# Attention of a two-layer diffusion backbone: two head pairs per step instead of one

## What is computed

```python
s_loc = jnp.einsum('bjqhd,bjlhd->bhjql', qr, kr).astype(jnp.float32) * scale + bias[None]
s_ctx = jnp.einsum('bjqhd,bnhd->bhjqn', qr, ctx_k).astype(jnp.float32) * scale
p = jax.nn.softmax(jnp.concatenate([s_loc, s_ctx], axis=-1), axis=-1)
o = jnp.einsum('bhjql,bjlhd->bjqhd', p[..., :L].astype(vr.dtype), vr)
o = o + jnp.einsum('bhjqn,bnhd->bjqhd', p[..., L:].astype(ctx_v.dtype), ctx_v)
```

## Time and profile before

| | before |
|---|---|
| median of 3 runs | 1589.21 us (1588.29 to 1589.9) |
| the profiled execution's own time | 1589.82 us |
| its span | 1588.0 us |
| TensorE busy (matmul, weight loads) | 99%, 87% |
| DVE, ACT, POOL busy | 83%, 49%, 25% |
| granted TensorE clock | 0.9 or more of full speed in all 40 slices |

### The profile page before, as it was taken

How to read it: one execution, slowest core, us unless ns; L and a number is a source line. 1 busy time by engine, 2 the same in 40 slices (tenths; PEclk the granted TensorE clock), 3 DMA queues, 4 the chain that set the end, 5 groups by cost and what they waited for, 6 DMA issues and landing times.

```text
span 1588.0 us, 28228 instructions
## 1 busy us (share of the span) xinstructions
PE 1567.4 (99%) x9688; PEld 1387.7 (87%) x9688; DVE 1313.5 (83%) x2295; ACT 772.5 (49%) x1443; POOL 389.5 (25%) x302
## 2 busy tenths in 40 slices
PE   7999999999999999999999999999999999999998
PEld 6788898789999999888878879977899999998886
DVE  7899787668999999966669987876699999998575
ACT  6433235538655555524383323363775555563333
POOL 0042012001555555300000600120035555541000
PEclk9999999999999999999999999999999999999999
DMA  9444375051222222454414444812412223235451
GB/s 363 140 131 158 99 270 164 14 146 54 79 81 79 85 88 85 152 161 163 149 40 146 142 131 155 276 61 87 76 66 80 83 89 92 80 93 180 126 186 66
DMA packets 66221, 195.05 MB, mean 123 GB/s; under 512 B 15444, under 2 KB 16852, under 8 KB 65880
## 3 DMA queue, kind: packets, MB, share of 16 engines
q1 hardware_dynamic: 50840, 175.54, 34.9%
q10 hardware_dynamic: 15296, 18.39, 3.6%
HBM read 187.05 MB, written 6.85 MB: 122 GB/s over the span
## 4 chain that ended last, share of the span: by engine, by line
PE 86%; DVE 7%; issue 3%; ACT 1%; DVEq 0%; ACTq 0%
PE bank L2155 12%; PE bank L2156 12%; PE bank L2157 12%; PE bank L2673 10%; PE bank L2674 10%; PE bank L2672 10%; PE bank L2311 2%; PE bank L2313 2%; PE bank L2315 2%; DVE ada_sq L1387 2%; PE bank L2467 2%; PE bank L2453 2%; DVE w_lo L1376 1%; PE bank L2177 1%; PE bank L2441 1%
## 5 line engine op out<-in xcount | busy, mean ns | idle before, releaser
L788 ACT ACTIVATE w_hi<-raw 128x1024 fp32r<-128x1024 f32 (+1 forms) x120 | 123.1, 1029 | 379.2 <-PE bank L2157 297.4
L1376 DVE TENSOR_TENSOR w_lo<-raw,w_hi 128x1024 fp32r<-128x1024 f32 (+1 forms) x128 | 154.3, 1213 | 113.6 <-ACT w_hi L788 113.2
L2155 PE MATMUL bank<-w_hi,aT_lo 128*128 128x512 f32 x520 | 210.3, 404 | 2.7 <-DVE aT_lo L1840 2.5
L2156 PE MATMUL bank<-w_lo,aT_hi 128*128 128x512 f32 x520 | 205.7, 396 | 0.0
L2157 PE MATMUL bank<-w_hi,aT_hi 128*128 128x512 f32 x520 | 205.2, 395 | 0.0
L2672 PE MATMUL bank<-aT_hi,w_lo 128*128 128x322 f32 x640 | 198.9, 311 | 0.7 <-DVE u L2020 0.7
L2673 PE MATMUL bank<-aT_lo,w_hi 128*128 128x322 f32 x640 | 199.4, 312 | 0.0
L2674 PE MATMUL bank<-aT_hi,w_hi 128*128 128x322 f32 x640 | 198.7, 310 | 0.0
L1268 ACT ACTIVATE w_hi<-raw 128x512 fp32r<-128x512 f32 x200 | 118.0, 628 | 147.4 <-POOL raw L668 139.4
L2155 PE MATMUL bank<-w_hi,m_lo 128*128 128x512 f32 x400 | 158.5, 396 | 0.0
L2156 PE MATMUL bank<-w_lo,m_hi 128*128 128x512 f32 x400 | 157.3, 393 | 0.0
(11 more groups left out here) (292 smaller groups left out, 3866.0 us busy)
## 6 DMA issues: line engine op xcount, KB each, us to landing
raw<-in_stream SPq DMA_DIRECT2D x304, 512.0 KB, 3.7
lead<-in_lead SPq DMA_DIRECT2D x16, 512.0 KB, 12.0
bias<-in_bias ACTq DMA_DIRECT2D x8, 896.0 KB, 10.4
na_v<-vn ACTq DMA_DIRECT2D x2, 1280.0 KB, 8.5
x<-in_xs SPq DMA_DIRECT2D x4, 512.0 KB, 13.7
vt<-na_v ACTq DMA_DIRECT2D x16, 128.0 KB
gb_mix<-gates ACTq DMA_DIRECT2D x2, 1024.0 KB, 4.5
gb_ffn<-gates ACTq DMA_DIRECT2D x8, 256.0 KB, 4.5
```

Source lines behind the costliest of these rows:

```text
L788: act.activation(w_hi[:, g % 4, 0:n], raw[:, s % 4, 0:n], ACT.Copy).then_inc(hi_done, 1)
L1376: dve.tensor_tensor(w_lo[:, g % 4, 0:n], raw[:, s % 4, 0:n], w_hi[:, g % 4, 0:n].bitcast(F32), ALU.subtract).then_inc(raw_free[s % 4], 1)
L2155: pe.matmul(out, ll, rh, start=start, stop=False)
L2156: pe.matmul(out, lh, rl, start=False, stop=False)
```

## The change

Step k now handles two units. TensorE: T(2k-2), T(2k-1), S(2k), S(2k+1), V(2k-2), V(2k-1), and the outputs of a group in odd steps from k = 3 (the last one in k = 10). ACT: the copies of bank 4 for both finished units, then the four exponentials of the next two, and in odd steps the high part of a group's output. DVE: the copies of bank 5 for both units, then both weighings, then the group's multiplication (odd k), or low part, reciprocal and copy-out (even k). Mix tiles 0 and 1 are transposed after S(1), tile 1 into bank 6 instead of 3; tiles 2 and 4 after the transposes of steps 1 and 2, tile 3 ahead of those of step 2. The low part of tiles 0 and 1 follows weigh(1), that of 2 the weighings of step 1, that of 3 stands between the two copies of step 2, and that of 4 follows its weighings. Weight 31 is split after the exponentials and weighings of step 2. In the last step the first part of out_products stands between T(18) and T(19). What each instruction computes is unchanged.

```diff
--- before.py
+++ after.py
@@ -453,7 +453,7 @@
 
         qk_blocks = [0, 1]
         MIX_TILES = (1, 2, 3, 4, 0)
-        MIX_BANKS = [7, 3, 7, 7, 7]
+        MIX_BANKS = [7, 6, 7, 7, 7]
         KQ_BANKS = [(4, 5), (6, 7), (0, 1), (2, 3), (4, 5), (0, 1), (2, 3), (6, 7)]
         NA_S = [(0, 1), (2, 3)]
         NA_T = (4, 5)
@@ -1186,25 +1186,32 @@
                         act.wait_ge(na_av, at(na_av, layer, u - 1))
                     act.activation(pt[:, u % 2, e, 0:n], bank[NA_T[e]][:, 0:n], ACT.Copy).then_inc(na_p, 1)
 
-                for i in range(NPU + 3):
-                    if i < NPU:
-                        exponentials(i, 0)
-                    if 1 <= i < NPU + 1:
-                        copy_transposed(i - 1, 0)
-                    if i < NPU:
-                        exponentials(i, 1)
-                    if i == 0:
-                        split_hi(30, layer)
-                        kq_evac(NB_IN - 1, 3, layer)
-                    if 1 <= i <= 4:
-                        mix_high((0, 1) if i == 1 else (i,), layer)
-                    if i == 4:
+                for k in range(NPU // 2 + 2):
+                    if k == 2:
+                        mix_high((3,), layer)
+                    if 1 <= k <= NPU // 2:
+                        copy_transposed(2 * k - 2, 0)
+                        copy_transposed(2 * k - 1, 0)
+                    if k == 1:
+                        mix_high((2,), layer)
+                    if k == 2:
+                        mix_high((4,), layer)
+                    for u in (2 * k, 2 * k + 1):
+                        if u < NPU:
+                            exponentials(u, 0)
+                            exponentials(u, 1)
+                        if u == 0:
+                            split_hi(30, layer)
+                            kq_evac(NB_IN - 1, 3, layer)
+                    if k == 0:
+                        mix_high((0, 1), layer)
+                    if k == 2:
                         split_hi(31, layer)
-                    if i == 18:
+                    if k == 9:
                         act.wait_ge(mod_done, at(mod_done, layer, MOD_ALL - 1))
                         store_gates(0, layer)
-                    if i >= 6 and i % 4 == 2:
-                        g = (i - 6) // 4
+                    if k >= 3 and k % 2:
+                        g = (k - 3) // 2
                         act.wait_ge(na_n, at(na_n, layer, g + 1))
                         src = nao[:, g % 2, :]
                         if g == HP:
@@ -1923,31 +1930,31 @@
                     if g == 29:
                         na_weigh(0, layer)
 
-                for i in range(NPU + 3):
-                    if 1 <= i < NPU:
-                        na_weigh(i, layer)
-                    if 2 <= i <= 5:
-                        mix_low((0, 1) if i == 2 else (i - 1,), layer)
-                    if i == 5:
+                for k in range(NPU // 2 + 3):
+                    if 1 <= k <= NPU // 2:
+                        copy_transposed(2 * k - 2, layer)
+                    if k == 2:
+                        mix_low((3,), layer)
+                    if 1 <= k <= NPU // 2:
+                        copy_transposed(2 * k - 1, layer)
+                    if 1 <= k < NPU // 2:
+                        na_weigh(2 * k, layer)
+                    if k < NPU // 2:
+                        na_weigh(2 * k + 1, layer)
+                    if k < 3:
+                        mix_low(((0, 1), (2,), (4,))[k], layer)
+                    if k == 2:
                         split_lo(31, layer)
-                    if 1 <= i < NPU + 1:
-                        copy_transposed(i - 1, layer)
-                    if i == 14:
+                    if k == 7:
                         dve.wait_ge(*freed(stream_ada(ADA_MIX - 1), layer))
                         times_gain(4 * KD, C_GF, 1.0, layer).then_inc(mod_done, 1)
                         times_gain(2 * KD, C_PM, 0.0, layer).then_inc(mod_done, 1)
-                    if i >= 5 and i % 4 == 1:
-                        g = (i - 5) // 4
-                        dve.wait_ge(na_e, at(na_e, layer, 2 * NQB * (g + 1)))
-                        dve.reciprocal(rec[:, g % 2, :], esum[:, g % 2, :]).then_inc(na_r, 1)
-                        dve.wait_ge(na_av, at(na_av, layer, NQB * (g + 1)))
-                        dve.tensor_copy(nao[:, g % 2, :], bank[NA_O[g % 2]][:]).then_inc(na_c, 1)
-                    if i >= 6 and i % 4 == 2:
-                        g = (i - 6) // 4
+                    if k >= 3 and k % 2:
+                        g = (k - 3) // 2
                         dve.wait_ge(mix_tp, at(mix_tp, layer, NT + g + 1))
                         dve.tensor_tensor(nao[:, g % 2, :], nao[:, g % 2, :], bank[NA_O[g % 2]][:], ALU.mult).then_inc(na_n, 1)
-                    if i >= 7 and i % 4 == 3 or i == NPU + 2:
-                        g = HP if i == NPU + 2 else (i - 7) // 4
+                    if k >= 4 and k % 2 == 0:
+                        g = (k - 4) // 2
                         dve.wait_ge(mix_hi, at(mix_hi, layer, NT + g + 1))
                         src = nao[:, g % 2, :]
                         if g == HP:
@@ -1958,6 +1965,12 @@
                                               src.rearrange("p (j r c) -> p j r c", j=NQB, c=CB),
                                               query_order(aT_hi[:, HP + g, P + GAP:MZ].bitcast(F32)),
                                               ALU.subtract).then_inc(mix_lo, 1)
+                    if 2 <= k <= NPU // 2 and k % 2 == 0:
+                        g = (k - 2) // 2
+                        dve.wait_ge(na_e, at(na_e, layer, 2 * NQB * (g + 1)))
+                        dve.reciprocal(rec[:, g % 2, :], esum[:, g % 2, :]).then_inc(na_r, 1)
+                        dve.wait_ge(na_av, at(na_av, layer, NQB * (g + 1)))
+                        dve.tensor_copy(nao[:, g % 2, :], bank[NA_O[g % 2]][:]).then_inc(na_c, 1)
 
                 for g, n in ((0, 2), (1, 2), (2, 1)):
                     split_lo(W_OUT0 + 4 + g, layer)
@@ -2408,9 +2421,7 @@
                     pe.wait_ge(ret_done, at(ret_done, layer, n + 1))
                     if n == 0:
                         pe.wait_ge(kq_T, at(kq_T, layer, 8))
-                    elif n == 1:
-                        pe.wait_ge(na_m, at(na_m, layer, 4))
-                    else:
+                    elif n >= 2:
                         pe.wait_ge(mix_lo, at(mix_lo, layer, 1 if n == 2 else n))
                     for a in range(HP):
                         i_ = pe.transpose(bank[MIX_BANKS[n]][:, a * P:(a + 1) * P], sg[:, tt, a * P:(a + 1) * P], ident[:])
@@ -2422,8 +2433,6 @@
                     pe.wait_ge(kq_T, at(kq_T, layer, 6 + u))
                 else:
                     pe.wait_ge(na_m, at(na_m, layer, 2 * u - 2))
-                if u == 3:
-                    pe.wait_ge(mix_lo, at(mix_lo, layer, 2))
                 if u >= 2 and PAIRS[u - 2][0] == HP:
                     pe.wait_ge(na_e, at(na_e, layer, 2 * u - 2))
                 outs = [bank[i] for i in NA_S[u % 2]]
@@ -2619,25 +2628,37 @@
                         if b > B_TOK and a == 2:
                             na_scores(0, layer)
 
-                for i in range(NPU + 3):
-                    if 1 <= i < NPU:
-                        na_scores(i, layer)
-                    if i == NPU:
+                for k in range(NPU // 2 + 1):
+                    two = (2 * k - 2, 2 * k - 1)
+                    if k == 0:
+                        na_scores(1, layer)
+                        mix_transposes((0, 1), layer)
+                        continue
+                    if k == 2:
+                        mix_transposes((3,), layer)
+                    na_transposes(two[0], layer)
+                    if 2 * k == NPU:
                         out_products(0, (0, 1), layer)
-                    if i == NPU + 2:
+                    na_transposes(two[1], layer)
+                    if k == 1:
+                        mix_transposes((2,), layer)
+                    if k == 2:
+                        mix_transposes((4,), layer)
+                    if 2 * k < NPU:
+                        na_scores(2 * k, layer)
+                        na_scores(2 * k + 1, layer)
+                    if k == 1:
+                        pe.wait_ge(v_moved, at(v_moved, layer, PER[v_moved]))
+                        pe.wait_ge(mix_lo, at(mix_lo, layer, 2))
+                    if k == 3:
+                        pe.wait_ge(mix_lo, at(mix_lo, layer, NT))
+                    na_values(two[0], layer)
+                    na_values(two[1], layer)
+                    if 2 * k == NPU:
                         out_products(0, (2, 3, 4), layer)
-                    if i == 2:
-                        pe.wait_ge(v_moved, at(v_moved, layer, PER[v_moved]))
-                    if 1 <= i < NPU + 1:
-                        na_transposes(i - 1, layer)
-                    if 2 <= i < NPU + 2:
```

(10 more changed lines are left out.)

## The result

The changed kernel took 1606.1 us (median of 5 runs, 1604.81 to 1607.18) against 1589.21 for the kernel before (five runs here too, in the range given there): 1.0107 times as long, 95% interval 1.0093 to 1.0121. It is slower, inside the range of 1594 to 1611 and 2.5 us over the predicted 1603.6. The profiled execution has a span of 1604.3 us, 16.3 more than before.

A forecast was written before the change was run, and what follows sets the result against it. TensorE's own order of work was taken as the bound, then a loop through ACT's queue: stage 50.8 + 6.5 + 9.5 = 66.8 against 59.6 us, 7.2 longer in each layer; 1589.21 + 14.4 = 1603.6; range 1594 to 1611.

The forecast's parts named there:

- The mechanism: Attention stage: transposes wait for bank copies queued behind ACT's exponentials and output copy; stage 7.2 us longer per layer.
- The loop's steps: Attention stage, from one step's second pair's transposes to the next's: even 5.30 us, odd 6.64, TensorE idle 0.9 and 1.3.
- the group: Four pairs with their outputs in the attention stage: 11.94 us against 10.82 before.
- The end: Attention stage after the loop: 6.5 us until pair 18's transposes end, then 9.5, nearly as before.
- The gaps: TensorE's gaps between scores and values or values and transposes: 0 to 0.33 us, -1.4 to +1.2 a layer.
- the clock: Rival: clock falls to 1.2 GHz where TensorE idles 1.3 us at a time; +20, 1620 us; chance 0.03.
- its likeliest case: Whole kernel: slower through the longer attention stage, 1598 to 1609 us; chance 0.65.
- Outside the stage: Work before and behind the attention stage: nothing found that gives time back; other changes costed at nothing.
- DVE isn't late: Even step: DVE's copy of the next first pair done at 5.4 us, wanted by second-head transposes at 5.6.
- only the bank counts: Rival: transposes wait only for the previous pair's bank copy, 0.54 us in each of ten steps; 1588 to 1590; chance 0.07.
- the opening alone: Rival: slower only by the stage's opening, 7.6 us over both layers, 1597; chance 0.15.
- the loop at par: Assumption of a rival: five steps of the attention stage at 5.41 us instead of 30.5 in all; 3.4 less a layer.

The follow-up runs named there:

- experiment 1: Changed kernel with only ACT's copy of a group's output moved behind the next step's two bank copies; 1603.41 us.
- experiment 2: Changed kernel with only the split of weight 31, on ACT and DVE, moved from step 2 to step 9; 1598.22 us.
- experiment 5: Changed kernel with ACT's output copy behind the next two bank copies, weight 31 split in step 9, and exponentials cut to 32 columns; 1593.58 us.
- experiment 8: Changed kernel with both pairs' scores between the two pairs' transposes, ACT's and DVE's queues reordered too, and weight 31 split in step 9; 1582.94 us.
- experiment 3: Changed kernel with every exponential cut to its first 32 columns, so results differ; run once, 1601.48 us.
- experiment 7: Changed kernel with 14 filling transposes ahead of each of pair 5's two transpose waits and 13 ahead of pair 1's first; 1602.73 us.
- experiment 6: Changed kernel with 14 filling transposes of the identity ahead of each of pair 5's two transpose waits; 1604.2 us.
- experiment 4: Changed kernel with ACT's output copy behind the next two bank copies and weight 31 split in step 9; 1594.82 us.

## Why the prediction held, step by step

**The mechanism was right.** T(b) directly behind T(a), one bank per head, and ACT's queue ahead of the copy: experiments 1 and 2 each took away one of the named stalls, experiment 5 measured what the bank alone costs, and experiment 8, whose order among other things undoes the adjacency, got below both kernels. The loop's steps were put at 5.30 and 6.64 and came out at 5.21 and 6.66, idle 0.9 and 1.3 against 0.78 and 1.35; the group 11.94 against 11.87, and what was left of it without waits 9.7 against 9.74. From T(b) of step 4 to T(b) of step 8 the sum was 23.9, and it took 311.65 - 287.91 = 23.74. The end took 16.2 against 16.0. T(5,e1) was forecast 20.56 us after scores(1) and came at 20.40, with the split of weight 31 ahead of it as said.

**The gaps** that no row had shown lie within their bounds of 0 to 0.33: 0.16 to 0.17 from T to S, 0.23 or 0.33 from S to V. The Trainium skill (TensorEngine Tiling (Array Packing), Key Properties) has the drain at a change of mode and not of tile. After agrees: the 16 matmuls of S(a') and S(b') follow each other without a gap, and the gaps of 0.16 to 0.33 us with nobody awaited stand where the form changes. What the rule leaves out is what decided here, that fewer changes of form put two users of one bank side by side.

**The term that was put at nothing: the clock.** From T(5,e1) to the outputs the changed kernel needed 4.93 us, 3.36 when the clock held (experiment 3): 1.57 a layer, 3.1 in all. The prediction had the fall as a rival at 0.03, at the wrong place (idle stretches of 1.3 us in the loop) and of the wrong size (+20 for a whole group at half). The loop's waits of 1.35 us, one in each odd step, didn't bring it down in the profiled execution (1.00 in the group's window); the opening's two of 1.5, with 0.52 us of transposes between, did, and the fall lasted 3.4 us. Without it the stage is 66.69 (experiment 7), and 66.8 was predicted. So the range held although its likeliest case had no term for the clock: its width covered the 3.1 us, which is luck and no part of the argument. The Trainium skill (TensorE: Matmul & The Clock Gate, Why this matters for your kernels) says that idle gaps between bursts bring the clock down. The trace agrees, with 0.51 at 281.00 to 283.40 after 0.52 us of work between 277.00 and 279.90, though each gap here is shorter than those it warns of. A wait of 1.5 us in a busy stage is thus to be priced with what comes behind it.

**Outside the stage** the sum had nothing. The span grew 16.3 where the stages grew 17.3, so about 1 us came back elsewhere: 0.47 ahead of the first stage, where the code is the same (scores(1) of layer 0 at 259.62 against 260.09), 0.12 between the two stages and 0.4 behind the second. In the other profiled executions the first stretch takes 259.30 to 260.72 and the last 491.6 to 492.7, so this is of the size by which executions differ, and no effect of the change. The miss of 2.5 us in the median is 3.1 for the clock, less some 1 for this, and small terms.

**"DVE isn't late" was true with nothing to spare.** In the even step of the changed kernel DVE's copy of bank 5 ended at 293.28 and T(b,e1) started at 293.48, of which some 0.15 is what a transpose takes to start behind a copy. It held there because ACT was later. As soon as ACT was relieved (experiments 1, 3 and 5), the second head's copy behind DVE's product or copy-out was what T(b,e1) waited for, for 0.08 to 0.18. This is why experiment 3 gained nothing in a group, and why the rival "only the bank counts", put at 1588 to 1590, came out at 1593.6 when its case was made (experiment 5): its 0.54 a step was 0.58, DVE adds 0.25 a group, and the opening stays 2.6 us later than before (first outputs at 20.68 against 18.12), which that rival had left out. The rival "the opening alone" had about the right size for the opening but not the loop at par, which nothing here reached with T(b) behind T(a): the least was 11.14 a group.

## What to carry to other kernels

Before grouping work by form to save TensorE's gaps, write down for each bank how long it takes from its first write to its release, here 0.59 us to the copy's start and 0.63 from there to the next transpose, and what TensorE has to do meanwhile that doesn't need the bank; one independent group of matmuls between two users (S between the two Ts) kept half of the gain in the gaps, 0.54 of 1.08 us a group, and none of the wait. Then read the copying engine's queue in the new order: whatever stands ahead of the copy, an output copy or a weight's split, is now in TensorE's loop, though its busy share is the same. An engine that is just "not late" is the next bound: here 0.20 us gained in the even step was followed by 0.18 lost in the odd one.

## What the runs showed of the hardware

- The granted clock fell to half for 3.4 us at T(5)'s waits of 1.5 us and 1.5 us, with 0.52 us of matmuls between them, in both layers of the changed kernel and in layer 0 of experiment 1. It did not in layer 1 of experiment 1, with the same two waits, where it had fallen and risen again earlier (1048.6 to 1052.0). Behind T(1)'s 1.60 and 0.41 us it fell in layer 1 of experiments 1 and 6, and not in the eight other layers with the same unfilled waits (both of the changed kernel and of experiments 2 and 4, one each of 1 and 6). It didn't fall behind 0.88 and 1.50 (experiment 3), nor anywhere with the waits filled. A fall behind T(5) costs 1.55 us, one behind T(1) 1.04 (first outputs at 24.81 against 23.77 in layer 1 of experiments 6 and 7). What else it depends on stays open.
- It shows in the times of single executions too: those of experiment 4, whose opening keeps T(1)'s long wait but not T(5)'s, were 1593.67 and 1594.12 us at a mean clock of 1.0, 1594.82 and 1596.38 at 0.998, and 1596.52 at 0.997. Of the changed kernel's five, four have 0.997, and the fastest, 1604.81 us, has 0.999. The same program does not lose the clock in the same way each time.
- 28 and 41 filling transposes a layer delayed nothing: the first outputs come at 23.78 and 23.77, and T(5,e1) at 20.41 us with 28 and 20.40 with none.
